# An SSD decay picked from running-sum rows, two reworked ends, and a new timetable for the attention heads

## The chip, the cores and the metric

The kernel runs on one core of a Trainium2 chip. Five engines work at once, each through its own list of instructions and strictly in order: TensorE (PE in the rows: matmuls and transposes, results into PSUM), VectorE (DVE), ScalarE (ACT), GpSimd (POOL) and SyncE (SP, which here only issues DMAs). They meet at semaphores. The metric is the device time of one execution in microseconds (us); the median of three runs of the kernel before is 2810.08 us (2809.82 to 2824.17).

## The reference

Two transformer-like blocks run one after the other on 256 tokens of width 2048, all in float32. Cut to what the change touches:

```python
# block 1, mixer: 32 heads of width 64 in 4 groups, state 128, one chunk of L = 256 tokens
a_cs = jnp.cumsum(dt * a, axis=token)                       # one running sum per head
decay = jnp.exp(jnp.where(causal, a_cs[l] - a_cs[s], -inf)) # L x L for each head
y = ((C @ B.T) * decay) @ (x * dt) + x * d_skip
h = h + mixer(h); h = h + cross_attention(h, mem)           # 4 heads of width 128
h = h + swiglu(h)
# block 2: 8 differential heads, 8 stick-breaking heads, 8 chunk-band heads
y = concat([diff(q_a, k_a, v_a), stick(q_b, k_b, v_b), band(q_c, k_c, v_c)])
x = x + y @ w_o; x = x + conv_swiglu(x)
return rmsnorm(x, final_norm)
```

A differential head takes two softmaxes and one value product; a stick-breaking head needs a reversed running sum along the keys and one exponential; a band head is a softmax over a window with a relative bias. All are followed by a norm per head.

## The kernel before

**The stream.** All weight matrices, 930 sub-units of 512 KB (128 x 1024 float32), are read once through four buffers (`raw`). ScalarE writes the rounded high part of each (`whi`, L819), VectorE the remainder (`wlo`, L1201), TensorE multiplies high by (high, low) of the activations and low by high. One step of the weight stream is a 512-column and a 256-column matmul; four steps make a **slot** and two slots use up one sub-unit. The program has 1860 slots. A stage (`su`, `xs`, `z`, `qa`, `va`, ... ) is a run of output tiles, each of 8, 16 or up to 32 steps, that alternate between two PSUM accumulators (`acc0`, `acc1`).

**The timetable.** Everything that isn't the weight stream is a task: a generator on each engine that is advanced by one `yield` per slot. `tasks()` says at which slot a task begins, and `idle(n)` inside a task how many slots it lets pass. So order on each engine is fixed when the program is built: a piece of a head sits between two slots of the stream, and if what it needs isn't ready, the engine stands still, with the rest of its stream behind it. TensorE does a slot's side pieces right after the slot's last matmul. ScalarE and VectorE handle a slot as follows: on odd slots first the split of a later sub-unit, then what leaves an accumulator, then the side pieces.

**The banks.** Four PSUM banks serve the tasks. `BANKS` gives for each use the first and last slot (counted from the task's begin) and the semaphore that frees it; `bank_table()` deals the banks out, and `take()` on TensorE waits for the previous user's semaphore. "Slack" below is the number of slots between the slot in which the producer's piece is listed and the slot in which TensorE waits for it.

**The decay.** `ssd(i)` runs at slot z+2+4i for heads 2i and 2i+1. The running sums are rebuilt for each head by multiplying a column of the step sizes `ADT` (high and low, two token halves), spread over 128 columns, with a triangle: eight matmuls (all matmuls are recorded at the helper, L477). ScalarE takes exp with a bias per row (L920, L921), VectorE multiplies by C B^T (L1313, L1314) and adds the skip term on two diagonals (L1317), and six slots later TensorE multiplies with x.

**Attention of block 2.** `dfa` (scores, softmax, transpose) and `dfb` (value product, norm) are the differential heads, `stk` two stick-breaking heads at a time, `bnd` two band heads at a time; `va`, `vb`, `vc` are the value projections, taken out of the accumulators by ScalarE (L1091). `dfb` waits for all four tiles of `va`, `stk` for both of `vb`, `bnd` for both of `vc`. Scores' banks are freed by the exponentials (L997 and L1065), those of the outputs by VectorE (L1438, L1474, L1497).

**The ends.** At the start ScalarE issues the DMA of the gains (`in_vec`, 16 columns) and the first two x tiles; then two scaled x tiles, the split of sub-unit 0, four x tiles, the next split. At the end norm 6 sums squares (L826), TensorE adds over partitions, and VectorE (12 tiles) and GpSimd (4) multiply x by gain and by 1/rms; four DMAs write the output.

## Time and profile before

| | before |
|---|---|
| median of 3 runs | 2810.08 us |
| profiled execution | 2806.39 us |
| its span in the trace | 2804.6 us |
| PE busy | 2757.1 us (98%) |
| DVE busy | 1952.7 us (70%) |
| ACT busy | 1284.8 us (46%) |
| POOL busy | 90.9 us (3%) |
| DMA queue q1, share of 16 engines | 52.5% |
| chain that ended last: PE at L477 | 94% |

The median is what is predicted; the profiled execution is the one whose rows are read. The span is the time between its first and last instruction. The chain is followed back from the last instruction, at each step to what released it. TensorE is nearly always busy, so what counts is how long its own list of instructions takes, and the few places at which it waits.

### The profile page before, as it was taken

Reading aid. Unit: us, or ns where it says so; the run is one execution under the profiler, and the core shown is the slowest. Engines: PE = TensorE matmul, PEld = TensorE weight load, DVE = VectorE, ACT = ScalarE, POOL = GpSimd, SP = SyncE. Lnnn points to the kernel's source line nnn. Section 1 sums busy time; section 2 is a strip of 40 time slices with the busy share of each in tenths; the row PEclk is TensorE's granted clock in tenths of the full one; section 3 lists DMA queues with packets and bytes.
Section 4 is the critical chain, followed back from the end, with each engine's and each line's share of the span. In section 5 each row is a group of like instructions: output and inputs, shape, how many; then the busy total and the mean of one; then the engine's idle time right before and its main releaser. Section 6 shows DMA issues by size and latency. Waiting matters only on the chain.

```text
span 2804.6 us, 40399 instructions
## 1 busy us (share of the span) xinstructions
PE 2757.1 (98%) x16796; PEld 2434.7 (87%) x16796; DVE 1952.7 (70%) x2416; ACT 1284.8 (46%) x1632; POOL 90.9 (3%) x67
## 2 busy tenths in 40 slices
PE   8999999999999999999999999999999999999997
PEld 7888999888888888888888888788898888888886
DVE  7777777766767665666566886576687757775775
ACT  5444545554555443444344544454454433443443
POOL 1000000000201000000000110000010000000002
PEclk9999999999999999999999999999999999999999
DMA  6555554346555555555555554344455555565553
GB/s 234 187 185 185 172 179 143 121 144 220 184 165 171 190 195 192 184 193 192 191 188 191 191 175 159 128 158 135 151 175 193 195 191 185 181 204 191 186 192 120
DMA packets 137622, 499.16 MB, mean 178 GB/s; under 512 B 15312, under 2 KB 16344, under 8 KB 137312
## 3 DMA queue, kind: packets, MB, share of 16 engines
q1 hardware_dynamic: 135792, 492.20, 52.5%
q10 hardware_dynamic: 1648, 4.39, 0.4%
q8 instruction: 132, 2.16, 0.3%
q14 instruction: 50, 0.41, 0.0%
HBM read 494.41 MB, written 2.11 MB: 177 GB/s over the span
## 4 chain that ended last, share of the span: by engine, by line
PE 94%; DVE 3%; ACT 2%; issue 0%; DMA 0%; DVEq 0%; ACTq 0%
PE PS L477 94%; DVE wlo L1201 1%; ACT whi L819 1%; DVE AR L1507 0%; DVE X L1635 0%; ACT AR L997 0%; DVE X L1677 0%; DMA X<-in_x 0%; PE PS L554 0%; DVE X L1633 0%; ACT AR L1065 0%; DVE H L1195 0%; DVE AR L1349 0%; DVE AR L1343 0%; DVE AR L1516 0%
## 5 line engine op out<-in xcount | busy, mean ns | idle before, releaser
L477 PE MATMUL PS<-H,whi 128*128 128x512 f32 (+1 forms) x5472 | 1787.0, 380 | 12.9 <-DVE wlo L1201 11.5
L1201 DVE TENSOR_TENSOR wlo<-raw,whi 128x1024 fp32r<-128x1024 f32 x930 | 1130.6, 1231 | 681.8 <-ACT whi L819 678.6
L819 ACT ACTIVATE whi<-raw 128x1024 fp32r<-128x1024 f32 x930 | 972.1, 1057 | 984.4 <-PE PS L477 956.3
L477 PE MATMUL PS<-H,wlo 128*128 128x256 f32 x5072 | 1413.8, 279 | 0.0
L477 PEld LDWEIGHTS PS<-H,whi 128*128 128x128 f32 x5472 | 1002.5, 188 | 220.8 <-issue 17.0
L477 PEld LDWEIGHTS PS<-H,wlo 128*128 128x128 f32 x5072 | 957.5, 189 | 2.0 <-issue 1.7
L477 PE MATMUL PS<-Y,whi 128*128 128x512 f32 (+1 forms) x2240 | 717.9, 376 | 1.1 <-DVE X L1635 0.8
L477 PE MATMUL PS<-Y,wlo 128*128 128x256 f32 x2048 | 569.0, 278 | 0.0
L477 PEld LDWEIGHTS PS<-Y,whi 128*128 128x128 f32 x2240 | 407.7, 188 | 83.9 <-DVE X L1635 2.0
L477 PEld LDWEIGHTS PS<-Y,wlo 128*128 128x128 f32 x2048 | 385.5, 188 | 0.2
L1507 DVE TENSOR_REDUCE AR<-PS 128x512 f32<-128x1024 f32 x140 | 171.5, 1225 | 14.6
L1687 POOL TENSOR_TENSOR AR<-AR 128x512 f32<-128x512 f32 x48 | 71.4, 1487 | 2033.3 <-ACT AR L826 2032.0
L804 ACT ACTIVATE AR<-AR 128x512 f32<-128x512 f32 x64 | 40.4, 632 | 209.1 <-DVE AR L1211 137.6
L477 PE MATMUL PS<-AR 128*128 128x256 f32 (+8 forms) x626 | 108.1, 352 | 13.5 <-ACT AR L997 3.4
L477 PE MATMUL PS<-whi,H 128*128 128x256 f32 x640 | 119.7, 288 | 0.0
L1184 DVE TENSOR_TENSOR AR<-AR 128x512 f32<-128x512 f32 x114 | 78.9, 692 | 35.0 <-ACT AR L804 32.6
L477 PEld LDWEIGHTS PS<-AR 128*128 128x128 f32 (+2 forms) x626 | 71.8, 175 | 36.1 <-issue 21.9
L477 PEld LDWEIGHTS PS<-whi,H 128*128 128x128 f32 x640 | 99.9, 191 | 2.3 <-issue 1.5
L1211 DVE SCALAR_TENSOR_TENSOR AR<-AR 128x255 f32<-128x255 f32 (+2 forms) x192 | 92.8, 484 | 6.8
L1129 ACT ACTIVATE Y<-AR 128x512 fp32r<-128x512 f32 x44 | 27.8, 632 | 149.4 <-DVE AR L1624 149.4
L477 PE MATMUL PS<-wlo,H 128*128 128x256 f32 x320 | 90.4, 283 | 0.0
L1193 DVE TENSOR_TENSOR Y<-AR,Y 128x512 fp32r<-128x512 f32 (+1 forms) x68 | 42.7, 628 | 38.2 <-ACT Y L1129 33.8
(160 smaller groups left out, 961.9 us busy)
## 6 DMA issues: line engine op xcount, KB each, us to landing
raw<-in_ffn SPq DMA_DIRECT2D x528, 512.0 KB, 4.4
raw<-in_w_in SPq DMA_DIRECT2D x178, 512.0 KB, 4.5
raw<-in_w_qkv SPq DMA_DIRECT2D x96, 512.0 KB, 3.8
raw<-in_w_out SPq DMA_DIRECT2D x64, 512.0 KB, 4.4
raw<-in_w_o SPq DMA_DIRECT2D x40, 512.0 KB, 3.8
raw<-in_w_q SPq DMA_DIRECT2D x8, 512.0 KB, 3.9
raw<-in_w_k SPq DMA_DIRECT2D x8, 512.0 KB, 3.8
raw<-in_w_v SPq DMA_DIRECT2D x8, 512.0 KB, 4.7
```

The costliest lines, as they stand in the source:

```text
L477: return e.matmul(out, l, r, start=start, stop=stop)
L804: return e.activation(dst, src, ACT.Silu)
L819: a.then_inc(e.activation(c.whi[:, s % NW, :], c.raw[:, s % NRAW, :], ACT.Copy), "whi")
L1129: a.then_inc(e.activation(c.hi("Y", 2 * (j - 8 * part), 2), two(q), ACT.Copy), "y_hi")
L1184: return e.tensor_tensor(two(dst), two(src), both(r), ALU.mult)
L1193: v.then_inc(e.tensor_tensor(c.lo(op, k, n), src, hi, ALU.subtract), made_)
L1201: v.then_inc(e.tensor_tensor(c.wlo[:, s % NW, :], c.raw[:, s % NRAW, :], c.whi[:, s % NW, :].bitcast(F32), ALU.subtract), "wlo")
L1211: v.then_inc(e.scalar_tensor_tensor(dst[:, sh:T], src[:, 0:T - sh], taps(width - 1 - sh), dst[:, sh:T], ALU.mult, ALU.add), name if sh == ...
L1507: v.then_inc(e.tensor_reduce(two(dst), c.acc[b].rearrange("p m (h t) -> p m t h", h=2), AX, ALU.add), f"acc{b}", turn + 1)
L1687: g.then_inc(e.tensor_tensor(c.SUM, c.SUM, c.SQ[i % 2], ALU.add), "sum_add")
```

## The change

**The decay.** The running sums of all 32 heads are now made once, as rows: in the task `dt`, after the old sums, four float32 matmuls write `row` (heads on partitions 0 to 31 and again on 32 to 63, 256 tokens along the free side). ScalarE rounds the first 64 rows to the high part, with the second token half repeated behind (`ACS`, 384 columns), VectorE overwrites partitions 32 to 63 with the low part, and `cr` clears the other 64. A selector `SEL` holds the identity of 32 in rows 0 to 31 and again in rows 32 to 63, so that one column of it, spread over 128, picks high plus low of one head. A decay is then two matmuls: the selector with `ACS`, and the mask for both diagonals in one.

On TensorE, the rows of the first decay step of the z stage, heads 0 and 1 (`SEL`, `ADT`, `CR` are the tables, H and whi/wlo the weight stream). Before:

```order
2446 L477 MATMUL PS<-H,wlo 128x256
2447 L477 MATMUL PS<-CR,ADT 128x384 [waits xs_copy,cr]
2448 L477 MATMUL PS<-CR,ADT 128x384
2449 L477 MATMUL PS<-CR,ADT 128x128 x4
2450 L477 MATMUL PS<-CR 128x128 x2
2451 L477 MATMUL PS<-CR,ADT 128x384 [waits xs_copy]
2452 L477 MATMUL PS<-CR,ADT 128x384
2453 L477 MATMUL PS<-CR,ADT 128x128 x4
2454 L477 MATMUL PS<-CR 128x128 x2
2455 L477 MATMUL PS<-H,whi 128x512
```

Now, on the same engine at the same place:

```order
2448 L476 MATMUL PS<-H,wlo 128x256
2449 L476 MATMUL PS<-CR,SEL 128x384 [waits xs_copy,cr]
2450 L476 MATMUL PS<-CR 128x2x128
2451 L476 MATMUL PS<-CR,SEL 128x384 [waits xs_copy]
2452 L476 MATMUL PS<-CR 128x2x128
2453 L476 MATMUL PS<-H,whi 128x512
```

Sixteen matmuls of a step have become four, and the two waits stay where they were.

**The timetable.** Begins of the tasks, in slots of the program:

| | before | now |
|---|---|---|
| xa 0..3 | 518, 520, 522, 524 | 511, 513, 519, 521 |
| dfa 0..7 | 1140, 1145, 1150, 1155, 1179, 1184, 1189, 1194 | 1140, 1147, ... 1189 (7 apart) |
| dfb 0..7 | 1173, 1177, 1181, 1185, 1196, 1200, 1204, 1208 | 1153, 1160, ... 1202 (7 apart) |
| stk 0..3 | 1208, 1213, 1234, 1239 | 1197, 1211, 1225, 1239 |
| bnd 0..3 | 1256, 1264, 1272, 1280 | 1245, 1254, 1264, 1276 |

`dfb`, `stk` and `bnd` now wait for the one tile of V (or of q and k) that holds their heads. Several `idle` counts grow by one, and `BANKS` keeps a bank one to three slots longer.

On TensorE, the value product of band heads 0 and 1 (four matmuls `PS<-AR 64x...`) and what stands around it. Before, inside the stage `ao1`, whose steps are 512 and 256 columns:

```order
10669 L477 MATMUL PS<-Y,whi 128x512 [waits y_made]
10670 L477 MATMUL PS<-Y,wlo 128x256
10671 L477 MATMUL PS<-AR 64x256 [waits acc0,bnd_copy]
10672 L477 MATMUL PS<-AR 64x128
10673 L477 MATMUL PS<-AR 64x256 [waits bnd_copy]
10674 L477 MATMUL PS<-AR 64x128
10675 L477 MATMUL PS<-Y,whi 128x512 [waits y_made]
```

Now, at the border between the first and second tile of the stage `vc`:

```order
10530 L476 MATMUL PS<-whi,H 128x256 x2
10531 L476 MATMUL PS<-wlo,H 128x256
10532 L476 MATMUL PS<-AR 64x256 [waits acc1,bnd_copy]
10533 L476 MATMUL PS<-AR 64x128
10534 L476 MATMUL PS<-AR 64x256
10535 L476 MATMUL PS<-AR 64x128
10536 L476 MATMUL PS<-whi,H 128x256 [waits wlo,acc0]
```

The product moved from four steps into `ao1`, where it waited for the second tile of `vc` (acc0), to directly behind the last matmul of the first tile, and waits for that tile (acc1).

**The start.** The gains are put in front of x, in one DMA of 528 columns; the first sub-unit comes as two halves that are split in turn with the first two x tiles; the table of the activation functions is asked for before the first wait. On ScalarE, its first rows. Before:

```order
1 L1154 DMA AR<-in_vec 128x16
2 L1155 DMA X<-in_x 128x512
3 L1151 ACT_TABLE_LOAD [waits x0]
4 L1151 ACTIVATE H<-X,AR 128x256 [waits gains]
5 L1151 ACTIVATE H<-X,AR 128x256
6 L819 ACTIVATE whi<-raw 128x1024 [waits raw0]
7 L1151 ACTIVATE H<-X,AR 128x256 [waits x1]
```

Now:

```order
1 L1162 DMA XG<-in_x 128x528
2 L798 ACT_TABLE_LOAD
3 L1160 ACTIVATE H<-XG 128x256 [waits x0]
4 L1167 ACTIVATE whi<-raw 128x512 [waits raw_first]
5 L1160 ACTIVATE H<-XG 128x256
6 L1170 ACTIVATE whi<-raw 128x512 [waits raw0]
7 L1160 ACTIVATE H<-XG 128x256 [waits x1]
```

Ahead of the first half of the weights there stand one x tile and half a split, where there were a table load, two x tiles and a whole one.

**The end.** ScalarE multiplies x by its gain as each tile of the last stage leaves, and loads the table for the last norm one tile early. Norm 6 starts three slots before the end: the matmuls over the partial sum go into the stream, those over the last squares stay behind it. After the norm VectorE multiplies six pairs of tiles by 1/rms, GpSimd two, and eight DMAs of 256 KB write the output.

The diff, cut to its core:

```diff
 def tasks():
-    out += [(first_slot("wv") + 2 + 2 * h, "xa", h) for h in range(4)]
+    out += [(first_slot("wv") + s, "xa", h) for h, s in enumerate((-5, -3, 3, 5))]
...
+    out += [(v + 7 * h, "dfa", h) for h in range(8)]
+    out += [(v + 7 * h + 13, "dfb", h) for h in range(8)]
+    out += [(v + s, "stk", i) for i, s in enumerate((57, 71, 85, 99))]
+    out += [(v + s, "bnd", i) for i, s in enumerate((105, 114, 124, 136))]
+    out += [(first_slot("g1") + 4, "norm", 5), (N_SLOT - 3, "norm", 6)]
 BANKS
-    "dfa": [("s0", 2, 5, "dif_exp", 2, 1), ("s1", 2, 5, "dif_exp", 2, 2), ("t", 11, 12, "dif_copy", 1, 1)],
+    "dfa": [("s0", 2, 6, "dif_exp", 2, 1), ("s1", 2, 6, "dif_exp", 2, 2), ("t", 11, 12, "dif_copy", 1, 1)],
-            ("t1", 9, 10, "bnd_copy", 2, 2), ("o", 12, 17, "bnd_y", 1, 1), ("n", 14, 15, "bnd_root", 1, 1)],
+            ("t1", 10, 12, "bnd_copy", 2, 2), ("o", 14, 20, "bnd_y", 1, 1), ("n", 16, 18, "bnd_root", 1, 1)],
 sync_program
+    e.dma_start(c.raw[:, 0, 0:half], c.d["w_in"][0][:, 0:half]).then_inc(c.sems["raw_first"], 16)
+    e.dma_start(c.raw[:, 0, half:SUB], c.d["w_in"][0][:, half:SUB]).then_inc(c.sems["raw0"], 16)
 tensor_program: norm, dt, ssd
+        last = norm_mm(bank, c.SUM, True, n != 6, n in (3, 4))
         if n == 6:
+            yield from idle(3)
             p.wait_ge("sq", 8 * n + 8)
+            last = norm_mm(bank, c.SQ[1], False, True, False)
...
+        row = bank[0:64, 128:384]
+        for o in (0, 32):
+            mm(row[o:o + 32, :], c.adt[:, 0:32], c.tri[:, 0:256], True, False)
+        for o in (0, 32):
+            last = mm(row[o:o + 32, 128:256], c.adt[:, 32:64], c.tri[:, 0:128], False, True)
...
-            mm(bank[:, 0:384], w0[0], c.TRIr, True, False)
-            mm(bank[:, 0:384], w0[1], c.TRIr, False, False)
-            for q in range(2):
-                for o in (128, 256):
-                    mm(bank[:, o:o + 128], w1[q], c.TRIr[:, 0:128], False, False)
-            mm(bank[:, 0:128], c.Ir, c.MNr, False, False)
-            p.then_inc(mm(bank[:, 256:384], c.Ir, c.MNr, False, True), "ssd_dec")
+            mm(bank[:, 0:384], c.SEL[:, h:h + 1].to_broadcast([P, P]), c.ACS, True, False)
+            ends = bank.rearrange("p (a b) -> p a b", a=2)[:, :, 0:128]
+            p.then_inc(mm(ends, c.Ir, c.MNr.unsqueeze(1).to_broadcast([P, 2, P]), False, True), "ssd_dec")
 tensor_program: dfb, stk, bnd
-        for j in range(4):
-            p.wait_ge(*done("va", j))
+        p.wait_ge(*done("va", h // 2))
...
-        for j in range(2):
-            p.wait_ge(*done("vc", j))
+        p.wait_ge(*done("vc", i // 2))
 scalar_program: dt, leave
+        a.then_inc(e.activation(c.ACS[0:64, 0:256], row, ACT.Copy))
+        a.then_inc(e.activation(c.ACS[0:64, 256:384], row[:, 128:256], ACT.Copy), "acs_hi")
...
+        if stage == "d12":
+            a.wait_ge(*a.at)
+            for k in (2 * j, 2 * j + 1):
+                a.then_inc(e.activation(c.xt(k), c.xt(k), ACT.Copy, scale=c.col("final_norm_2", k)), "scaled")
+            if j == 6:
+                load(LN_EXP)
 vector_program: dt, ssd, end
+        low = c.ACS[32:64, :]
+        v.then_inc(e.tensor_tensor(low[:, 0:256], bank[32:64, 128:384], low[:, 0:256].bitcast(F32), ALU.subtract))
...
-            for o in (0, 256):
-                v.then_inc(e.scalar_tensor_tensor(E[:, o:o + 128], c.ident, c.col("d_skip", h), E[:, o:o + 128], ALU.mult, ALU.add),
+            diag = two(E)[:, :, 0:P]
+            v.then_inc(e.scalar_tensor_tensor(diag, c.ident.unsqueeze(1).to_broadcast([P, 2, P]), c.col("d_skip", h), diag,
+                                              ALU.mult, ALU.add), "ssd_e")
...
-    for k in range(16):
-        if k % 4:
-            v.then_inc(e.scalar_tensor_tensor(c.xt(k), c.xt(k), c.col("final_norm_2", k), c.RN, ALU.mult, ALU.mult), "gain_x")
+    for i in range(6):
+        v.wait_ge("scaled", 2 * i + 2)
+        v.then_inc(times(c.xt(2 * i, 2), c.xt(2 * i, 2), c.RN), "gain_x")
 gpsimd_program: end
+    for i in (6, 7):
+        x = two(c.xt(2 * i, 2))
+        g.then_inc(e.tensor_tensor(x, x, both(c.RN), ALU.mult), "pool_x")
```

## Rows read from the trace of the kernel before

**Rows 1.** Busy us of each engine in four stretches (start:end, length, engines).

```profile
1640.00:1700.00 60.00, 58.70 (x336) 50.81 (x335) 42.91 (x54) 25.04 (x27) 1.52 (x1) 1.00 0.60 200
1700.00:2000.00 300.00, 285.43 (x1907) 250.97 (x1906) 189.35 (x339) 146.22 (x291) 0.00 (x0) 0.99 0.42 140
2786.30:2804.60 18.30, 1.97 (x8) 1.44 (x8) 9.84 (x18) 2.74 (x4) 7.24 (x8) 0.70 0.28 115
443.30:581.40 138.10, 138.10 (x892) 118.81 (x891) 102.62 (x196) 83.70 (x125) 0.00 (x0) 1.00 0.36 122
```

**Rows 2.** Timeline of TensorE, decay step (start, us, instruction, count).

```profile
468.77 0.91 PE L477 MATMUL PS<-CR,ADT 128*128 128x384 f32 x6
...
469.74 0.96 PE L477 MATMUL PS<-CR,ADT 128*128 128x384 f32 x6
...
470.76 0.44 PE L477 MATMUL PS<-H,whi 128*128 128x512 f32 x1
```

**Rows 3.** Timeline of TensorE, two 384-column matmuls and what follows them.

```profile
1713.56 0.52 PE L477 MATMUL PS<-CR 128*128 128x384 f32 x2
1714.01 0.93 PE L477 MATMUL PS<-AR 64*128 64x128 f32 x8
```

**Rows 4.** Timeline of TensorE, a 256-column matmul and the next start.

```profile
360.04 0.28 PE L477 MATMUL PS<-H,wlo 128*128 128x256 f32 x1
360.16 0.40 PE L477 MATMUL PS<-H,whi 128*128 128x256 f32 x2
```

**Rows 5.** Timeline of TensorE, four plain f32 matmuls and the next start.

```profile
572.86 1.89 PE L477 MATMUL PS<-AR 128*128 128x256 f32 x8
574.39 1.09 PE L477 MATMUL PS<-CR,ADT 128*128 128x384 f32 x6
```

**Rows 6.** Timeline of the start, all engines.

```profile
6.92 1.28 ACT L1151 ACT_TABLE_LOAD   x1 [6.92 <-DMA X<-in_x]
...
8.22 0.91 ACT L1151 ACTIVATE H<-X,AR 128x256 fp32r<-128x256 f32 x2
...
10.11 1.23 DVE L1201 TENSOR_TENSOR wlo<-raw,whi 128x1024 fp32r<-128x1024 f32 x1 [0.38 <-ACT whi L819]
...
11.48 0.77 PE L477 MATMUL PS<-H,whi 128*128 128x512 f32 x1 [11.48 <-DVE wlo L1201]
```

**Rows 7.** Waits of TensorE: total us, times, longest us.

```profile
PE PS L477 <- ACT AR L997: 6.5, 5, 2.0
PE PS L477 <- DVE AR L1497: 3.1, 2, 2.2
...
PE PS L477 <- DVE AR L1460: 1.6, 1, 1.6
PE PS L638 <- ACT AR L811: 1.4, 1, 1.4
...
PE PS L605 <- DVE AR L1349: 1.0, 1, 1.0
```

**Rows 8.** Timeline around the value product of band head pair 0.

```profile
1944.54 1.06 ACT L819 ACTIVATE whi<-raw 128x1024 fp32r<-128x1024 f32 x1 [3.01 <-PE PS L477]
...
1946.47 0.88 PE L477 MATMUL PS<-AR 128*64 128x256 f32 x8 [0.62 <-ACT AR L1091]
```

**Rows 9.** Granted clock of TensorE (the column PEclk) in one stretch of four us.

```profile
1784.00:1788.00 4.00, 4.00 (x20) 0.66 0.33 115
```

**Rows 10.** Timeline of the end.

```profile
2787.04 0.69 DVE L1635 TENSOR_TENSOR X<-X,PS 128x512 f32<-128x512 f32 x1
...
2788.53 1.97 PE L477 MATMUL PS<-AR 128*128 128x256 f32 x8 [2.25 <-ACT AR L826]
...
2791.04 1.28 ACT L799 ACT_TABLE_LOAD   x1 [2.66 <-DVE AR L1215]
...
2794.61 6.71 DVE L1677 SCALAR_TENSOR_TENSOR X<-X,AR 128x256 f32<-128x256 f32 x12
2794.66 3.61 POOL L1720 TENSOR_TENSOR X<-X,AR 128x256 f32<-128x256 f32 x4 [2.55 <-DVE AR L1224]
```

More of the change, by code:

```diff
@@ L719, in bnd @@
             p.then_inc(last, "bnd_turn")
-        yield from idle(3)
+        yield from idle(4)
         bank = take("bnd", i, "o")
-        for j in range(2):
-            p.wait_ge(*done("vc", j))
+        p.wait_ge(*done("vc", i // 2))
         for n, WT in enumerate((P0, P1)):
@@ L841, in norm @@
         _, r, col = norm_dst(c, n)
-        yield
+        yield from idle(3 if n == 6 else 1)
         if col is not None:
```

179 lines of the change are left out of this document (90 added, 89 removed).

## The prediction

> **What bounds the kernel now.** I read first the page's engine totals and its chain, then the busy time by stretches, then who TensorE waited for, and last the timelines at the places that the change touches. TensorE is the bound: in the z stage, where the decays are made, it is busy for all of 138.1 us, VectorE for 102.62 and ScalarE for 83.70 [rows 1]. So there a microsecond less in TensorE's list is a microsecond less in the time. Its idle time sits in four places. It starts at 11.48 us [rows 6]. In the 300 us of attention in block 2 it is busy for 285.43, and in the 60 us before for 58.70: 14.6 and 1.3 us idle [rows 1]. In the 18.3 us behind the last matmul of the stream it works 1.97 us [rows 1]. And it waits 1.0 us once in the cross attention [rows 7]. All of this counts in full, since nothing else keeps the end away.
>
> **The decay.** A step makes two heads. Its 16 matmuls stand between 468.77 and 470.76, so 1.99 us, or 1.02 us for the second head alone (469.74 to 470.76) [rows 2]. What takes their place are a 384-column matmul and one of 256 columns for each head. Two 384-column matmuls took 0.45 us to the next start, 0.225 each [rows 3]; a 256-column one took 0.12 us [rows 4]. That makes 0.345 a head, 0.69 a step, and saves 1.30 us. There are 16 steps: 20.8 us. The new forms (one column of the selector as weights, a mask written to two pieces of the bank) aren't in the trace. The weights of before were one column spread as well, so there I see no risk. The mask could cost as much as the two 128-column matmuls that it replaces: six small matmuls took (1.02 - 0.45) = 0.57 us, 0.095 each, so 0.19 instead of 0.12, and over 32 heads 2.2 us less gained (18.6). At the other end each 384-column matmul costs what 256 columns cost plus half, 0.18: 1.4 us more (22.2). I take 20.8.
>
> Here a rule weighs in. The removed 128-column matmuls took 0.095 us each, though 128 of 256 columns should be half of 0.12. The Trainium skill (TensorE: Matmul & The Clock Gate, LDWEIGHTS) says that the weight load lasts by the number of weight columns alone, 107 ns for 128, whatever the matmul behind it is. The trace agrees roughly, with 95 ns. By columns alone the 896 that go for each head would be worth 896 x 0.12 / 256 = 0.42 us, 13.4 us in all; by the rule with the rows it is the 20.8. I go by the rows, which have the removed step whole.
>
> Added once: four plain f32 matmuls of 256, 256, 128 and 128 columns. Four of 256 lasted 1.53 us (572.86 to 574.39) [rows 5], so three quarters of that, 1.15 us, and not below 0.36, what 768 columns cost in the other format [rows 4]. The two copies on ScalarE and three small operations on VectorE beside them lie forty slots ahead of the first decay, one slot being about 1.5 us (2804.6 us over 1860 slots), and cost nothing. VectorE loses one of two skip operations a head. If the stage shrinks to 118.5 us, its 102.62 are 87%: high, but six slots lie between the exponential and the product with x. Net: -19.6 us.
>
> **The attention of block 2.** What TensorE waited for by name: five times an exponential of the differential heads, 6.5 us, the longest 2.0; twice the last operation of a band head, 3.1; a masked logarithm 1.6; a root 1.4 [rows 7]. I counted the slack of every such wait in both timetables. Before, 13 waits on task semaphores have a slack of one slot or none: six on those exponentials (the scores of a head take a bank that the head before has just used), two on roots, five on the last operation of a head. Five slots apart is too near for a softmax chain. Now the heads are seven slots apart, the exponentials at +5 free banks that are taken at +9, and not one of these has a slack below two. One slot more is about 1.5 us, more than the mean of the five waits (1.3). So these go, but not all: the longest wait on a band head, 2.2 us, had a slack of one and now has two, and keeps some 0.8; the masked logarithm waited 1.6 with a slack of three, because VectorE was behind, and its load over these slots stays (four stick pairs, now partly beside the band heads). I keep 1.5 there. The 1.3 us before slot 1140 are in slots that the change leaves alone; they stay.
>
> And one wait is new. The product of band heads 0 and 1 now stands directly behind the last matmul of the first `vc` tile, slack nought. ScalarE first splits a sub-unit on this slot, then empties the accumulator. Before, the same pair of operations stood in front of the same product: from the split's start to the product it took 1944.54 to 1946.47, so 1.93 us, of which TensorE idled only 0.62 since it had four steps between [rows 8]. Now it has none: I charge 1.9 us. Behind it in TensorE's list stands the rest of the stream, so it is paid in full.
>
> Idle left: 1.3 + 1.9 + 0.8 + 1.5 = 5.5 of 15.9 us, gain 10.4. Behind the longest gap (2.0 us) the granted clock was 0.66 over four us [rows 9], 1.4 us of full clock lost; if no gap is as long, that comes back too, though the new one of 1.9 us may bring it again. Together -11.8 us. Bounds: all gaps go, -16; the kept and new ones double, -5.
>
> **Cross attention.** The transposes get one more slot behind the weights of the softmax: the wait of 1.0 us [rows 7] goes. What follows there, the short waits of `xo` on VectorE, isn't touched. -1.0 us, between 0 and -2.
>
> **The start.** x is there at 6.92, then a table load of 1.28, two x tiles 0.91, a split on ScalarE (1.06 [rows 8]) and on VectorE (1.23) [rows 6] lead to 11.48. Now: no table load, one x tile 0.46, halves 0.53 and 0.62, and some 0.2 of passing on: 8.75, so -2.7 us. The second halves and x tiles follow each other closely enough to keep a starting TensorE fed. Bounds: only the table load, -1.3; the DMA of x also comes half a microsecond earlier, being issued first, -3.3.
>
> **The end.** The table load of 1.28 us stands in the chain and goes [rows 10]. VectorE's 12 tiles took 6.71 us; six 512-wide operations at 0.69 are 4.1: -2.6. GpSimd did four tiles in 3.61 [rows 10], so two pairs take no more than that and end first. Of the four matmuls in 1.97 us two move into the stream: -1.0 behind it, and +0.77 in it (half of 1.53 [rows 5]). ScalarE's new multiplications for the last tile lie beside these matmuls. Sum -4.1 us. Bounds: the queue of eight DMAs eats half, -2; the last transfer is half as large, -5.
>
> **Sum.** 19.6 + 11.8 + 1.0 + 2.7 + 4.1 = 39.2 us. The profiled execution took 2806.4, which gives 2767.2; the median of the runs shown is 3.7 us above that execution, so I predict 2771 for the median.
>
> **Rivals.**
> 1. The z stage finds a new bound in VectorE. For it: 87% busy in long bursts beside a strict order. Against: no wait there had a slack under two slots in either timetable. If VectorE can't be packed beyond 80%, the stage lasts 102.62 / 0.8 = 128.3 and not 118.5 us: 2781.
> 2. The waits of attention move and don't go. VectorE must do the same work in about the same slots, and a band pair or stick pair that is late costs in a new place. If all 15.9 us stay and the 1.9 come on top, and the clock drop stays, the 11.8 turn into +1.9: 2785.
> 3. Slower than before. The new timetable has some 75 waits of TensorE with a slack of two or three slots between slots 1142 and 1292. If VectorE falls more than two slots behind there for the whole stretch, each of them costs. From a mean of (39.2 + 2.3) / 75 = 0.55 us on, the gain is gone; at 0.8 us it is 2771 + 60 - 2.3 = 2829. Against: VectorE was busy for 189.35 of 300 us [rows 1], 63%, and the heads are now spread more evenly, so its backlog should be smaller than before.
> 4. The ends give nothing, because the first transfers and the last ones set the time and not the engines: 2771 + 6.8 = 2778.
>
> **Chances.** The forecast 0.75; rival 1 0.06, rival 2 0.12, rival 3 0.02, rival 4 0.05. The range 2760 to 2784 takes the bounds of the parts together (not all at the same end) and nearly reaches the full loss of attention. Half a percent is 14 us, about what a measurement can tell from no change: everything but rival 3 is below 2796. Faster 0.96, same 0.02, slower 0.02.
>
> **What would show it.** TensorE's decay steps should stand 0.6 to 0.75 us from their first matmul to the next weight step, and the stage should have no idle time. In attention the waits on the exponentials should be absent, a single wait of about 1.9 us should stand before the product of band heads 0 and 1, with ScalarE's copy of the accumulator as releaser, and idle time should be near 4 us between slots 1140 and 1300. The first matmul should start near 8.8 us. Behind the last weight step no table load should appear, and 14 us should remain. I am wrong if the z stage shows idle TensorE, if the waits on VectorE in the stick and band heads sum to more than 6 us, or if the first matmuls are followed by gaps.

## The result and the profile after

| | before | after |
|---|---|---|
| median (4 runs each) | 2817.12 us | 2786.65 us |
| range | 2809.82 to 2824.58 | 2786.13 to 2787.81 |
| profiled execution, its span | 2806.39, 2804.6 | 2786.13, 2784.3 |
| PE busy | 2757.1 us | 2748.0 us |

The ratio of the times is 0.990, with a 95% interval of 0.987 to 0.993. I had forecast 2771, in a range of 2760 to 2784. The kernel is faster, but the time lies above the range. The span shrank by 20.3 us where my sum has 39.2. (The medians differ by 30.5 us, since two of the four runs before are at 2824.)

The stretches of [rows 1], cut at the same slots, in the changed kernel (columns as there):

```profile
442.42:558.89 116.47, 115.42 (x699) 95.61 (x698) 95.54 (x163) 82.42 (x126) 0.00 (x0) 1.00 0.44 144
1617.78:1676.44 58.66, 57.86 (x336) 50.52 (x334) 42.52 (x54) 24.70 (x27) 1.20 (x1) 1.00 0.62 204
1676.44:1967.69 291.25, 282.71 (x1905) 250.03 (x1904) 188.82 (x338) 146.51 (x292) 0.00 (x0) 0.99 0.44 144
2768.70:2784.30 15.60, 1.42 (x6) 0.68 (x4) 8.96 (x12) 2.37 (x5) 3.43 (x2) 0.64 0.36 135
```

The z stage went from 138.1 to 116.5 us, more than forecast. The attention, 360 us before, takes 349.9, and what lies behind the last step 15.4 instead of 18.3 (the fourth stretch above begins 0.25 us before that step ends). These, the start and the cross attention already give more than the 20.3. So something took time in stages that the change doesn't touch. I took the start time of each of the 7440 steps of the weight stream from both traces and laid them on each other, slot by slot:

| slots | what is there | forecast | after minus before, us |
|---|---|---|---|
| first matmul | start | -2.7 | -3.4 |
| 0 to 240 | start, `su`, `sc`, ... | | +1.7 |
| 240 to 280 | running-sum rows | +1.15 | +0.9 |
| 280 to 360 | decay | -20.8 | -21.7 |
| 385 to 452 | `wo1`, `wo2`: not touched | 0 | +1.8 |
| 480 to 552 | cross attention | -1.0 | -1.9 |
| 552 to 1080 | first feed-forward stage | 0 | 0.0 |
| 1080 to 1320 | attention of block 2 | -11.8 | -9.5 |
| 1337 to 1859 | second feed-forward stage | +0.8 (norm 6) | **+14.7** |
| behind the last step | end | -4.9 | -3.0 |

One row holds the miss. The second feed-forward stage isn't touched but for norm 6 at its end, TensorE doesn't wait in it in either trace, and yet it is 14 us longer. In a window of 500 us inside each feed-forward stage, the number of matmuls (x behind the second number) tells how fast the stream goes. Before:

```profile
1000.00:1500.00 500.00, 500.00 (x2886) 437.22 (x2885) 315.96 (x300) 203.76 (x211) 0.00 (x0) 1.00 0.57 190
2200.00:2700.00 500.00, 500.00 (x2886) 437.25 (x2885) 353.75 (x390) 201.63 (x209) 0.00 (x0) 1.00 0.56 188
```

After:

```profile
1000.00:1500.00 500.00, 500.00 (x2886) 437.16 (x2885) 316.29 (x300) 203.76 (x211) 0.00 (x0) 1.00 0.58 190
2200.00:2700.00 500.00, 500.00 (x2831) 433.63 (x2830) 346.36 (x379) 198.86 (x207) 0.00 (x0) 1.00 0.56 185
```

Both are busy for 500 of 500 us at a granted clock of 1.00, but in the second stage TensorE gets through 2831 matmuls instead of 2886. A step lasts 346.7 ns there before and 353.3 after (start of slot 1400 to start of slot 1600, 800 steps: 277.33 and 282.66 us). TensorE's timeline shows how. Before, the starts of the 512-column matmuls are always 0.35 apart:

```profile
2199.90 0.40 PE L477 MATMUL PS<-H,whi 128*128 128x512 f32 x1
2200.13 0.28 PE L477 MATMUL PS<-H,wlo 128*128 128x256 f32 x1
2200.25 0.39 PE L477 MATMUL PS<-H,whi 128*128 128x512 f32 x1
...
2200.59 0.40 PE L477 MATMUL PS<-H,whi 128*128 128x512 f32 x1
```

After, they go 0.35, 0.36, 0.35, 0.35, 0.36, so one step of three is longer:

```profile
2199.80 0.40 PE L476 MATMUL PS<-H,whi 128*128 128x512 f32 x1
...
2200.15 0.40 PE L476 MATMUL PS<-H,whi 128*128 128x512 f32 x1
...
2200.51 0.40 PE L476 MATMUL PS<-H,whi 128*128 128x512 f32 x1
...
2200.86 0.40 PE L476 MATMUL PS<-H,whi 128*128 128x512 f32 x1
```

I call this the fast and the slow cadence. A step is one such pair, the 512- and the 256-column matmul. In both traces the cadence changes only where a side piece of TensorE (a norm's matmuls, for instance) breaks the stream, and holds until the next one. The feed-forward stages are 527 and 523 slots without a side piece, so one such change is worth 527 x 4 x 6.66 ns = 14.0 us. It is taken up behind norm 2 (slot 552) and norm 5 (slot 1336). Slots 385 to 452 show the same: the +1.8 us.

The other readings, step by step. The decay step (before: [rows 2]) has its four matmuls between 464.94 and 465.53, 0.59 us, just under the 0.6 to 0.75 that I expected:

```profile
464.94 0.34 PE L476 MATMUL PS<-CR,SEL 128*128 128x384 f32 x1
465.12 0.28 PE L476 MATMUL PS<-CR 128*128 128x256 f32 x1
465.23 0.34 PE L476 MATMUL PS<-CR,SEL 128*128 128x384 f32 x1
465.42 0.28 PE L476 MATMUL PS<-CR 128*128 128x256 f32 x1
465.53 0.39 PE L476 MATMUL PS<-H,whi 128*128 128x512 f32 x1
```

TensorE's waits (total, times, longest; before: [rows 7]):

```profile
PE PS L715 <- DVE AR L1511: 3.4, 2, 2.8
PE PS L476 <- ACT AR L1094: 3.3, 2, 2.7
...
PE PS L476 <- DVE AR L1455: 1.8, 1, 1.8
...
PE PS L559 <- ACT AR L803: 1.1, 1, 1.1
```

The five waits on exponentials (6.5 us) and the root (1.4) are gone; the masked logarithm (L1455) waits 1.8 us, where I kept 1.5. The new one before the product of band heads 0 and 1 (L1094) is there, with 2.7 us for my 1.9. Unforeseen are two. One is 2.8 us on the band weights (L1511) at 1952.63. The other stands in the z stage, which I had said would have no idle time: behind the first decay step TensorE waits 1.05 us for ScalarE (L803, a silu that the last transposes of x need), which loads a function table (1.28 us) between the exponentials and this silu. TensorE now comes to it 1.4 us earlier, and `ssd_only` below has the same wait. The timeline of the wait on L1094, answering to [rows 8]:

```profile
1895.45 0.48 ACT L1068 ACTIVATE AR<-PS,AR 128x256 f32<-128x256 f32 x1
...
1895.90 1.06 ACT L818 ACTIVATE whi<-raw 128x1024 fp32r<-128x1024 f32 x1
1896.85 0.84 ACT L1094 ACTIVATE AR<-PS,AR 128x256 f32<-128x256 f32 x2
...
1897.84 0.88 PE L476 MATMUL PS<-AR 128*64 128x256 f32 x8 [2.71 <-ACT AR L1094]
```

From the split's start to the product it is 1.94 us, as in [rows 8]. The rest of the 2.71 is that ScalarE came to the split late: it was still at the band's exponentials (L1068). Behind each of the two long waits stands half a clock, as behind the gap of before ([rows 9]; PEclk is the number behind the busy times):

```profile
1898.00:1902.00 4.00, 4.00 (x23) 3.58 (x22) 0.23 (x1) 0.39 (x1) 0.00 (x0) 0.64 0.41 131
1953.00:1957.00 4.00, 3.86 (x16) 3.25 (x15) 1.61 (x3) 0.82 (x2) 0.00 (x0) 0.60 0.35 121
```

The start (before: [rows 6]):

```profile
6.21 0.51 ACT L1160 ACTIVATE H<-XG 128x256 fp32r<-128x256 f32 x1 [3.74 <-DMA XG<-in_x]
6.63 0.61 ACT L1167 ACTIVATE whi<-raw 128x512 fp32r<-128x512 f32 x1
...
8.11 0.77 PE L476 MATMUL PS<-H,whi 128*128 128x512 f32 x1 [8.11 <-DVE wlo L1680]
...
9.96 0.91 ACT L1160 ACTIVATE H<-XG 128x256 fp32r<-128x256 f32 x2 [1.00 <-DMA XG<-in_x]
...
13.22 0.47 PE L476 MATMUL PS<-H,whi 128*128 128x512 f32 x1 [0.51 <-DVE wlo L1215]
```

The first matmul starts 3.4 us earlier, but ScalarE then waits for x at 9.96 and TensorE for the next split at 13.22 (0.51 us), and again at 33.52 (0.48 us), so that half of it is lost by slot 40. The end (before: [rows 10]):

```profile
2771.15 1.13 PE L476 MATMUL PS<-AR 128*128 128x256 f32 x4 [2.16 <-ACT AR L825]
...
2775.11 5.83 DVE L1198 TENSOR_TENSOR XG<-XG,AR 128x512 f32<-128x512 f32 x6
2775.16 3.43 POOL L1744 TENSOR_TENSOR XG<-XG,AR 128x512 f32<-128x512 f32 x2 [12.04 <-DVE AR L1238]
```

VectorE's six last operations take 5.83 us, where I had 4.1.

### The profile page after: what moved, and what is told of

It is laid out like the page before. It is cut to its first block, busy times and chain, and to the rows that moved or that the text cites. A ratio compares the mean times of both kernels' runs of the same rounds, so it can differ in the third digit from the quotient of the medians.

```text
span 2784.3 us, 40021 instructions
## 1 busy us (share of the span) xinstructions
PE 2748.0 (99%) x16612; PEld 2417.8 (87%) x16612; DVE 1946.7 (70%) x2382; ACT 1289.5 (46%) x1650; POOL 86.6 (3%) x61
## 3 DMA queue, kind: packets, MB, share of 16 engines
q10 hardware_dynamic: 1792, 4.91, 0.5%
## 4 chain that ended last, share of the span: by engine, by line
PE 94%; DVE 3%; ACT 1%; DMA 1%; issue 0%; POOL 0%; DVEq 0%; ACTq 0%; POOLq 0%
PE PS L476 94%; DVE wlo L1215 1%; ACT whi L818 1%; DMA raw<-in_w_in 1%; DVE XG L1415 0%; POOL AR L1713 0%; DVE XG L1652 0%; DVE AR L1524 0%; DMA XG<-in_x 0%; DVE AR L1225 0%; DVE XG L1198 0%; PE PS L559 0%; ACT AR L1068 0%; DVE H L1209 0%; DVE XG L1650 0%
## 5 line engine op out<-in xcount | busy, mean ns | idle before, releaser
L1524 DVE TENSOR_REDUCE AR<-PS 128x512 f32<-128x1024 f32 x140 | 171.5, 1225 | 14.9 <-PE PS L476 0.5
L803 ACT ACTIVATE AR<-AR 128x512 f32<-128x512 f32 x64 | 40.4, 632 | 209.6 <-DVE AR L1225 137.9
```

Of the source, the lines that this page charges most:

```text
L803: return e.activation(dst, src, ACT.Silu)
L1524: v.then_inc(e.tensor_reduce(two(dst), c.acc[b].rearrange("p m (h t) -> p m t h", h=2), AX, ALU.add), f"acc{b}", turn + 1)
```

## The experiments

The main theory: the missing 14 us are the cadence, which a side piece of TensorE sets. Against it stood that something lasting slows the stream in that stage (transfers, memory places, other engines), and that my terms were wrong. "Kicks" below are small matmuls whose result nobody reads.

**1. The kernel before again.** No edit.

> The kernel before, unchanged. Theory 1 (two cadences): a step of the weight stream lasts 346.7 or 353.3 ns, one of the two is taken up at each side piece of TensorE and kept until the next, and in the two long stretches without side pieces (slots 553 to 1080 and 1337 to 1859, the two feed-forward networks) this makes 14.0 and 13.9 us. Then this kernel's own runs differ among themselves by about 14 us (2810 or 2824), and if the profiled run is one of 2824, its trace shows 353.3 ns in one of the two stretches and nothing else different. Theory 2 (the change made the second network slower, by its layout of x or its DMAs): runs of this kernel have 346.7 ns in both stretches always, and their spread has another cause.

Measured: 2807.75 to 2824.46 in ten runs, in two groups, 2807.75 and 2807.97, and 2820.06 to 2824.46. Over all comparisons of this study the kernel before ran 69 times: 18 runs at 2803 to 2812, 44 at 2819 to 2826, 7 at 2834 to 2837. The groups are 14 us apart, what one feed-forward stage is worth. Its profiled runs (2806.4, 2807.8) belong to the lowest group, with both stages fast. No run of the upper groups was profiled, so that they are the slow cadence is not read from a trace of this kernel; experiment 12 bears on it.

**2. Kicks in the changed kernel**, in the feed-forward stages behind every 16th slot, in fp32r in the first stage and in plain f32 in the second (`Ir` and `ones` are tables):

```diff
+for first, last, at, ws in ((564, 1076, 2, (16, 32, 64, 128)), (1348, 1852, 5, (1, 16, 64, 128))):
+    if first <= t < last and (t - first) % 16 == 0:
...
+        w = ws[(t - first) // 16 % 4]
+        x, l = (c.Ir[:, 0:w], c.Ir) if at == 2 else (c.ones[:, 0:w], c.ones)
+        mm(bank[:, 0:w], l, x, True, True)
```

> The kernel after, with one small matmul, whose result nobody reads, behind every 16th slot of the two feed-forward networks: in the first network fp32r of 16, 32, 64, 128 columns in turn, in the second plain f32 of 1, 16, 64, 128 columns in turn, 32 in each. Theory 1: the duration of a step changes between 346.7 and 353.3 ns at some of these matmuls, in both networks and in both directions, and is constant between two of them. Theory 2: the first network stays at 346.7 and the second at 353.3 ns throughout, but for the matmuls themselves.

Measured: 2805.62 us. In the first stage the cadence changes at the kicks, both ways, and holds in between; its pattern of eight kicks repeats exactly four times (fast, fast, fast, slow, slow, slow, fast, slow for widths 16, 32, 64, 128 twice). In the second stage it stays slow behind all 32. Around a kick of 128 columns the timeline shows the change, a step of 0.35 ahead of it, and from 941.77 on 0.35, 0.36, 0.35:

```profile
940.62 0.39 PE L476 MATMUL PS<-H,whi 128*128 128x512 f32 x1
...
940.97 0.40 PE L476 MATMUL PS<-H,whi 128*128 128x512 f32 x1
941.20 0.28 PE L476 MATMUL PS<-H,wlo 128*128 128x256 f32 x1
941.32 0.22 PE L476 MATMUL PS<-CR 128*128 128x128 f32 x1
941.37 0.44 PE L476 MATMUL PS<-H,whi 128*128 128x512 f32 x1
...
941.77 0.40 PE L476 MATMUL PS<-H,whi 128*128 128x512 f32 x1
...
942.12 0.40 PE L476 MATMUL PS<-H,whi 128*128 128x512 f32 x1
...
942.48 0.40 PE L476 MATMUL PS<-H,whi 128*128 128x512 f32 x1
...
942.83 0.40 PE L476 MATMUL PS<-H,whi 128*128 128x512 f32 x1
```

In the first stage a matmul changes it, with the same transfers, memory and engines on both sides, so there what lasts is ruled out. The second stage, where the miss is, stayed slow as theory 2 had it; its answer came with experiments 6 and 8.

**3 and 4. The parts alone, on the kernel before.** `ssd_only` has the decay's edits only, `timetable_only` those of the timetable, waits and banks.

```diff
 # 3
-            w0 = [c.ADT[:, 2 * q, h:h + 1].to_broadcast([P, P]) for q in range(2)]
...
+            mm(bank[:, 0:384], c.SEL[:, h:h + 1].to_broadcast([P, P]), c.ACS, True, False)
 # 4
-    out += [(v + s, "dfa", h) for h, s in enumerate((0, 5, 10, 15, 39, 44, 49, 54))]
+    out += [(v + 7 * h, "dfa", h) for h in range(8)]
```

> The kernel before with the decay of the change alone. By the slots of the trace: the z stage (slots 280 to 360) shorter by 20 to 22 us, slots 200 to 280 longer by 0.9 to 1.2 us, no idle TensorE in the z stage. Theory 1: whatever cadence the two networks take (a multiple of 14 us in the total) has nothing to do with the z stage. Rival (VectorE as a new bound in the z stage): less than 15 us.

> The kernel before with the timetable, waits and banks of the change alone. By the slots of the trace: slots 1080 to 1320 shorter by 8 to 10 us as in the trace of the kernel after (9.5), 4 to 9 us of idle TensorE there, with a wait of 2 to 3 us on the first vc tile before the product of band heads 0 and 1. Theory 2 (the start of x and its layout set the second network's pace): 346.7 ns a step there. Theory 1: either cadence can come.

Measured: 2784.89 and 2827.33 us. The first has both feed-forward stages fast, the second both slow, as its windows say:

```profile
1000.00:1500.00 500.00, 500.00 (x2832) 433.49 (x2831) 310.62 (x294) 198.12 (x205) 0.00 (x0) 1.00 0.57 187
2200.00:2700.00 500.00, 500.00 (x2833) 433.57 (x2831) 346.34 (x379) 198.27 (x206) 0.00 (x0) 1.00 0.57 187
```

So the timetable alone looks 21 us slower than the profiled execution of before, and is faster in every stage that it touches: by slots, -8.6 us from 1104 to 1320 and -1.3 in the cross attention, against 28 lost to the cadence and 2.7 more by slot 240, where nothing is changed. The decay alone is +0.9 and -21.7 us, as in the whole. It brings 3.1 us more, between slots 1180 and 1220, where it doesn't change anything: no half-clock stretch is recorded in this run, before the end, where the kernel before has two (3.41 us each). One costs 1.55 us, then.

**5. The ends alone**, on the kernel before.

```diff
-    for k in range(0, 16, 4):
-        s.wait_ge("gain_x", k + 4 - k // 4 - 1)
+    for i in range(6):
+        s.wait_ge("gain_x", i + 1)
...
+    a.then_inc(e.activation(c.whi[:, 0, 0:half], c.raw[:, 0, 0:half], ACT.Copy), "whi_first")
```

> The kernel before with the start and the end of the change alone (weights at the head of the queues, gather of the constants, norm 6 in the stream, short last additions); decay and attention timetable as before. The cadence of the weight stream is read apart, from the steps of slots 553 to 1080 and 1337 to 1859: 346.7 or 353.3 ns each, at 14 us a stage. With it taken out: my prediction expects -2.7 us at the start and -4.1 at the end, so a span of 2798 with both stages fast. What the two traces showed already says about -1.6 at the start (the first matmul 3.4 earlier, but then a gap at 13 us while ScalarE still waits for the input) and -3 at the end (15.3 us behind the last matmul in place of 18.3), so 2800. Rival: the start is worth nothing, since the stream catches on the input either way: at slot 40 the two stand equal and the span is 2802 or more.

Measured: 2808.91, span 2807.1: longer than before. The first matmul is 3.2 us earlier and what lies behind the last step 3.5 shorter. But by slot 40 2.1 are given back, and 4.0 more by slot 240, where the stages `su` and on stand in the slow cadence (353.4 ns from slot 31 to 174). Norm 6's matmuls add 0.9, a third half-clock stretch 1.5 between slots 1220 and 1320, and the cross attention is 0.8 longer. As a total it is inconclusive; by places it supports what the two traces said.

**6. Two kicks of 64 columns** in the changed kernel, which had left the fast cadence behind them 8 times of 8.

```diff
+    table = {556: 64, 1340: 64}
...
+        if t in table:
...
+            mm(bank[:, 0:w], c.Ir, c.Ir[:, 0:w] if w <= 128 else c.CR[:, 0:w], True, True)
```

> The changed kernel with two unread matmuls of 64 columns (fp32r), one behind slot 556 and one behind slot 1340, nothing else. Theory 1 (the miss is the slow cadence in the second feed-forward stage; a 64-column matmul has left the fast one behind it 8 times of 8): slots 1341 to 1859 go at 346.7 ns a step, 519 x 4 x 6.66 ns = 13.8 us less; slots 557 to 1080 are fast in every run; time 2772 to 2773, all runs within 1 us of each other. Theory 2 (the slow cadence in that stage comes from something that lasts: the transfers, the other engines, the place in memory of the buffers that the change moved): it stays 353.3 and the time 2786 to 2787. Theory 3 (the cadence is taken up by chance at each side matmul): some runs at 2772, some at 2786 and some at 2800.

Measured: 2773.40, 2788.94, 2773.52, 2785.51. The profiled run (2773.4) has both stages at 346.7 ns, and the second stage is 13.7 us shorter than in the changed kernel. That the miss was this, is shown. But two runs of four are 12 and 15 us above: two kicks don't hold it.

**7. The band tasks later, with the same two kicks.**

```diff
-    out += [(v + s, "bnd", i) for i, s in enumerate((105, 114, 124, 136))]
+    out += [(v + s, "bnd", i) for i, s in enumerate((109, 120, 126, 138))]
```

> As k64, and the four band tasks of the attention begun 4, 6, 2 and 2 slots later, so that band 0's value product comes 4 slots behind the last matmul of vc tile 0 instead of right behind it. If TensorE's waits of 2.71 us (at 1897.8) and 2.78 us (at 1952.6) in the changed kernel are a matter of these places, both go or fall under 0.5 us, and with them perhaps the two half-clock records behind them: 5 us from the waits and up to 3.2 from the clock, so 2764 to 2768. If the second wait is VectorE's own row of work (residual additions and splits ahead of the band weights), the first goes alone: 2769 to 2770. Rival: the later bands push their last product against the second half of the output projection and the time is that of k64 or above (2772 to 2776).

Measured: 2764.80, 2780.60, 2777.67, 2765.59. From slot 1080 to 1320 it is 8.6 us shorter than with the kicks alone. Of the two waits 0.6 us each is left, and no half-clock stretch is recorded before the end:

```profile
PE PS L715 <- DVE AR L1522: 0.6, 1, 0.6
PE PS L476 <- ACT AR L1105: 0.6, 1, 0.6
```

So both waits were a matter of places, the second too. The half-clock stretch behind the second wait went with it (7.1 of the 8.6 us lie between slots 1220 and 1320). The rest is another such stretch, at 1755, ahead of the band tasks: experiment 6 has it, this run doesn't, and experiments 10 and 11 with the same band tasks have it again, so it isn't theirs.

**8. A survey of kicks.** 110 in the changed kernel: in the first stage 128 columns and, 6 to 11 slots later, 64; in the second 8 to 112 columns out of each cadence.

```diff
+    table = {556: 128, 562: 64, 570: 128, 577: 64, 585: 128, 593: 64, ..., 1344: 128, 1353: 8, 1362: 128, 1371: 16, ...}
```

> The changed kernel with 110 unread fp32r matmuls: in the first feed-forward stage a 128-column one (slow cadence behind it, 8 of 8 before) and 6 to 11 slots later a 64-column one, so that it meets the slow pattern of three steps at each of its three places; in the second stage 8, 16, 24, 32, 40, 48, 56, 64, 72, 80, 96 and 112 columns, each once out of the slow cadence and once out of the fast one. Theory A (the cadence behind a side matmul follows from its width alone): the same answer from both and at every distance; 64 fast always. Theory B (it follows from width and from where in its pattern the stream stands): 64 gives slow for at least one of the three places, and some widths give fast from fast and slow from slow. Theory C (chance): repeats at the same distance disagree. Time 2786 to 2800, not of interest.

Measured: 2798.09. In the pattern of twelve kicks the 64-column ones leave the fast cadence behind them four times and the slow one twice, the 128-column ones the slow one four times and the fast one twice, and this is the same in all five whole repetitions. So neither width has an answer of its own: width and place decide together, and within a run nothing looks like chance (theory B). In the second stage 16, 24, 32, 40, 48 and 56 columns left the fast cadence fast (each once); 72, 80, 96 and 112 didn't, 8 did once of twice, and 64 six times of seven.

The traces allow a sharper test of theory B. The slow pattern has three places, and the fast cadence runs in two ways, with steps of 344 and 350 ns in turn or of 346 and 347. Over the 186 kicks of fp32r in the feed-forward stages of eight runs (`kicks`, `kicks2`, `k64`, `k64_bnd` and the four with 32 columns), sorted by their width and by where the stream stood ahead of them, each of the 36 combinations that occur was always followed by the same cadence (16 of them occur more than once, with 166 of the kicks). Out of the slow one, 64 columns gave fast at two of the three places (16 and 13 times) and slow at the third (5 times); out of the fast one, slow behind steps of 344 and 350 ns (6 times) and fast behind steps of 346 and 347 (17 times). 32 columns left the fast one fast 40 times of 40, and ended the slow one at two of its three places.

**9. The changed kernel again.** No edit.

> The changed kernel itself, unchanged, in more executions. If each of the two feed-forward stages is at random in the fast or the slow cadence (14 us each), its times fall into groups 14 us apart: 2772 to 2774 with none slow, 2786 to 2788 with one, 2800 to 2802 with both, as those of the kernel before do (2803 to 2811, 2819 to 2825, 2834). If the changed kernel always takes up the slow cadence in the second stage and never in the first, as its first four runs (2786.1 to 2787.8) would have it, no run lies under 2785 or above 2789.

Measured: 2785.74 to 2788.55 four times, 2800.51 and 2801.69. The profiled run is that of 2800.51, and has both stages slow:

```profile
1000.00:1500.00 500.00, 500.00 (x2833) 433.54 (x2832) 310.67 (x295) 198.08 (x204) 0.00 (x0) 1.00 0.57 186
2200.00:2700.00 500.00, 500.00 (x2832) 433.66 (x2831) 346.58 (x379) 197.93 (x206) 0.00 (x0) 1.00 0.57 186
```

The same program, another execution, 14 us more: groups, as with the kernel before. By their times none of the ten runs of the changed kernel had both fast.

**10. The band tasks later, without kicks** (the diff of 7 on the changed kernel).

> The changed kernel with the four band tasks begun 4, 6, 2 and 2 slots later and no unread matmuls. With them the same shift took 8.4 us off the stretch from slot 1080 to 1320 (waits of 2.7 and 2.8 us and both half-clock records gone). Theory: those 8.4 us do not hang on the unread matmuls, so each group of times lies 8.4 lower than in the changed kernel: 2764, 2778 or 2792. Rival: a third of them was the place of the clock's window and comes back: 2767, 2781.

Measured: 2779.81, 2779.77, 2792.93, 2791.73, each group 7 to 9 us below that of the changed kernel. One half-clock stretch is recorded here: some of the 3.1 us come and go.

**11. Twenty kicks of 32 columns, bands later.** Those at the head of each feed-forward stage are 4, 5, 6 and 5 slots apart, so that they meet the slow pattern at each of its places; the rest of the stage is left alone.

```diff
+    table = {556: 0, 560: 0, 565: 0, 571: 0, 576: 0, 1340: 1, 1344: 1, 1349: 1, 1355: 1, 1360: 1, 387: 1, 391: 1, 396: 1, 402: 1, 456: 0, 460: 0, 465: 0, 1107: 2, 1111: 2, 1116: 2}
...
+        if t in table:
+            mm(c.misc[table[t]][:, 0:32], c.Ir, c.Ir[:, 0:32], True, True)
```

> The changed kernel, the band tasks later, and unread fp32r matmuls of 32 columns: five at the head of each feed-forward stage (4, 5, 6 and 5 slots apart, so that they meet the three-step pattern of the slow cadence at each of its places), four from slot 387, three from slot 456, three from slot 1107. In the last survey 16 to 56 columns left the fast cadence fast 7 times of 7, and 32 changed the slow one to the fast one at some of its places. Theory (phase decides, and a kick that meets the right place ends the slow cadence for good): every run in the lowest group, 2761 to 2765, spread under 2 us; 20 kicks cost 0.02 to 0.1 us each, 1.8 + 0.9 us come back from the slow stretches of slots 385 to 488 and 0.9 from 1105 to 1142. Rival (chance at each kick): groups 14 us apart remain, some runs at 2776 or more.

Measured: 2763.31 to 2765.38 in six runs, median 2764.83. The groups are gone. In the profiled run both feed-forward stages are entered slowly (353 ns a step up to slots 556 and 1340) and go fast from the first kick on. A kick costs 0.12 us, more than I expected: the steps around it begin 375, 433 and 352 ns apart instead of 346.7.

**12 and 13. The same twenty kicks in the kernel before and in the changed one** (bands as they were).

> The kernel before with the same twenty unread fp32r matmuls of 32 columns at the same slots. Theory (its two groups of times, 2804 to 2811 and 2819 to 2825, are one feed-forward stage in the slow cadence or none): the upper group goes, and every run lies at 2804 to 2808: its fast profile (2806.4) plus some 1 us for the matmuls, minus 0.9 us for slots 1105 to 1142, which it goes through slowly. Rival (the kernel before has another source of its upper group, and the matmuls only suit the changed kernel): runs above 2815 remain.

> The changed kernel, band tasks as they were, with those twenty matmuls: all runs in one group at 2772 to 2774 (the version with later bands, 2763.3 to 2765.4, plus 8.4 us). Against the kernel before with the same matmuls this is the change without the cadence: my sum says 2767 - 2806 = -39, the slots of the profiled runs say about -33 (decay -20.9, attention -9.0, cross attention -2 to -3, start +1.6 at slot 40 against a first matmul 3.4 earlier, end -3).

Measured: before 2809.55 us (2805.95 to 2811.32, 12 runs) while the kernel before without them ran at 2809 to 2837 on the same chip; after 2773.28 (2771.67 to 2776.35, 6 runs). Both profiles are fast in both stages; that of the changed kernel:

```profile
1000.00:1500.00 500.00, 500.00 (x2886) 440.84 (x2885) 316.37 (x301) 203.63 (x211) 0.00 (x0) 1.00 0.56 190
2200.00:2700.00 500.00, 500.00 (x2886) 440.88 (x2886) 353.70 (x386) 202.91 (x210) 0.00 (x0) 1.00 0.56 191
```

The kernel before is 2 us slower than I expected of it: twenty kicks cost 2.4 us and not 1, and in its profile 1.9 us more have gone by slot 240, where `su` stands in the slow cadence for longer. Each of the two profiles has two half-clock stretches before the end. With the cadence held, the change is worth 36.3 us, against the 39.2 of my sum.

**14. The end on VectorE alone**, on top of 11.

```diff
-    for i in range(6):
+    for i in range(8):
         v.wait_ge("scaled", 2 * i + 2)
         v.then_inc(times(c.xt(2 * i, 2), c.xt(2 * i, 2), c.RN), "gain_x")
...
-    for i in (6, 7):
-        x = two(c.xt(2 * i, 2))
-        g.then_inc(e.tensor_tensor(x, x, both(c.RN), ALU.mult), "pool_x")
```

> The last version (twenty 32-column matmuls, later bands) with all eight last multiplications on VectorE and none on GpSimd; ScalarE issues two of the eight output transfers as before. In the profile of the changed kernel VectorE's six took 5.83 us, two of them 1.75 us each while GpSimd did its two (3.43 us), the others 0.68. Theory: VectorE is slowed by GpSimd's work beside it, so that GpSimd's help costs more than it brings: eight at a start-to-start of 0.60 us are 4.9 us, none above 0.75, 0.9 us less at the end, time near 2763.9. Rival: the two slow ones were held by something else at the head of the row (the transfers that begin, the gains), so the second and third stay at 1.75 and eight take 7.1 us, 1.3 us more: 2766.

Measured: 2762.75 (2762.50 to 2764.26, 4 runs). VectorE's last operations (duration ns: least, median, most), first in the changed kernel:

```profile
L1198 DVE TENSOR_TENSOR XG<-XG,AR x6: 677/686/1750, 2775.1 to 2780.3; 128x512 f32<-128x512 f32 x6
```

Without GpSimd at work beside it:

```profile
L1207 DVE TENSOR_TENSOR XG<-XG,AR x8: 684/685/692, 2752.0 to 2756.2; 128x512 f32<-128x512 f32 x8
```

Eight alone take 4.91 us, six beside GpSimd 5.83. From the start of the last step of the stream to the end it is 15.3 us instead of 16.5 in experiment 11. (The median fell by 2.1 us; 1.55 of the difference between the two profiles is a half-clock stretch less, in slots that the edit doesn't touch.)

This last version is the best of all: its ratio to the kernel before is 0.981 (0.977 to 0.985), and it lies 24 us under the changed kernel's 2786.65.

## Why the prediction missed

**The step that failed** is the sum's base: "The profiled execution took 2806.4, which gives 2767.2; the median of the runs shown is 3.7 us above that execution". It took every stage that the change leaves alone at its time in one profiled execution, and the 14 us between the runs shown (2809.82 and 2824.17) for noise with a median. That execution had both feed-forward stages in the fast cadence; by their times so had 18 of 69 runs of that kernel, while the usual run (44 of 69) pays for one slow stage, and so did each of the four runs of the changed kernel in the comparison (the profiled one by its trace). Runs 6, 9 and 11 to 13 show it: held fast, the changed kernel takes 2773.28, 2 us above my forecast; left alone, the same program gives 2786 or 2800. With the cadence held in both, -36.3 us stands for -39.2. No rival had this; rival 2's time (2785) is nearly the one measured, for a wrong reason, since the waits did go.

The terms, from experiments 12 and 13 in slots (us, forecast in brackets): start up to slot 240 -3.4 (-2.7), of it 1.2 a cadence in `su`; rows and decay +0.9 and -21.7 (+1.15 and -20.8); cross attention -1.4 (-1.0); attention -8.6 (-11.8); end, with norm 6's matmuls in the stream, -1.7 (-4.1). They sum to the -36.1 between the two spans with 0.2 left for the rest.

- **Decay: right**, 0.9 too careful: 0.59 us a step for 0.69. By removed columns alone it would have been 13.4 us. The rows, which had the removed step whole, are borne out by the 21.7. The Trainium skill (TensorE: Matmul & The Clock Gate, LDWEIGHTS) has a weight load last by its number of weight columns alone. The trace agrees in so far as kicks of 16, 32 and 64 columns, each with 128 weight columns, take the same 0.145 us from the matmul ahead to the next of the stream; that the weight load is the cause, no run here shows. VectorE, 95.5 of 116.5 us, isn't the bound, so rival 1 is out. But "no idle time", which I had named as a test, failed by the 1.05 us at the silu; the steps themselves gave 1.4 us each, so 22.7 in all.
- **Attention: the mechanism right, the size 3 us off.** Idle in the two stretches [rows 1] went from 15.9 to 9.3 us; I had 5.5. The wait for `vc` took 2.7 for 1.9, since I priced it from a place where ScalarE was free in time. The band weights (2.8) weren't in the sum: a slack of three slots, which I took as safe, wasn't, because VectorE had the output projection's additions ahead in its row. And the 1.4 us of clock didn't come back: two half-clock stretches before, of which [rows 9] showed one, and two after, behind the two new gaps. Run 7 shows that both were the task's places.
- **Cross attention: right.** Its wait is absent.
- **Start: the chain right, its sequel not.** 3.4 us came at the first matmul and 1.7 went by slot 240. I had named gaps behind the first matmuls as what would show me wrong.
- **End: the step "six 512-wide operations at 0.69 are 4.1" failed.** It took the duration of such an operation while GpSimd rests; 1.7 of the 2.4 us that are missing lie here. [rows 10] had the warning: VectorE's 12 tiles were recorded beside GpSimd's four, so their mean mixed two durations. Run 14 shows it. The Trainium skill (GPSIMD Engine Reference, Specifications) states the cause in general, that GpSimd shares its SBUF interfaces with VectorE and that VectorE's instructions with two SBUF inputs contend with it; this multiplication has two, and the trace agrees, with 1.75 us beside 0.68.

What stays open: why an execution takes up the one cadence or the other. Within a run it follows from the widths and places of what breaks the stream, but the changed kernel and `kicks` part in slot 489 with the same list of instructions before it. Whether the change makes the fast cadence rarer (none of ten runs had both stages fast, against 18 of 69) isn't shown. And how the half-clock stretches fall isn't settled: with gaps alike in the attention of block 2, `ssd_only` has none, the kernel before two and `ends_only` three.

## What to carry to other kernels

Before you sum up what a change saves, look at how the runs of the unchanged kernel spread: two groups of times are two behaviours of the program, and a profile shows one of them. Compare two traces by the starts of the same instructions, all along, not by busy time: TensorE was 100% busy at full clock in both cadences. And price an operation from a row where its neighbours do what they will do afterwards: VectorE's time beside a working GpSimd, ScalarE's wait behind its own row.

## What the hardware showed that I had not expected

- A stream of 512- and 256-column fp32r matmuls, each with its own 128-column weights, has two cadences at full clock: 346.7 ns a pair, or 353.3 in a pattern of three pairs. At 2.4 GHz that is 832 and 848 periods. Each holds for up to 527 slots (2108 pairs) without a break; one fp32r matmul between two steps can switch it, and 64 and 128 columns did so both ways, by where in its pattern the stream stood.
- Kicks of 32 columns, spaced so that they meet each place of the slow pattern, took the upper groups away in all 28 runs of the four kernels that had them; a kick costs 0.12 us, of which 0.03 lie before the next matmul of the stream (0.145 us from the matmul ahead of it, where 0.117 stands without) and the rest in the two steps behind.
- A half-clock stretch of 3.41 us in the clock record costs 1.55 us, and came behind gaps of TensorE of 1.4 to 2.8 us, though not behind all of them.
- VectorE's 512-column multiplication took 1.75 us while GpSimd multiplied, and 0.68 alone.
